# Inverse roots spread by two DMAs through a row in device memory, in place of products with the identity

## The chip, the cores and the metric

The kernel runs on one core of a Trainium2 chip. The metric is the device time of one execution in microseconds; the profile adds the span from the first to the last instruction of a profiled execution. The core has TensorE (PE, with its weight loads as PEld), VectorE (DVE), ScalarE (ACT), GpSimd (POOL) and SyncE (SP), which here only issues DMAs.

## The reference

Two residual layers over x of 512 positions by 1024 channels. Layer 0 is windowed attention, layer 1 is retention with four heads, and each ends in a gated MLP with a causal convolution of width 3. What matters here is where a norm stands:

```python
def rmsnorm(x, g):
    y = xf * lax.rsqrt(jnp.mean(xf * xf, axis=-1, keepdims=True) + EPS)
    return (y * g.astype(jnp.float32)).astype(x.dtype)
...
def retention(h, w_in, w_o):
    q, k, v, g = jnp.split(h @ w_in, [R_QK_COLS, 2 * R_QK_COLS, 2 * R_QK_COLS + R_V_COLS], axis=-1)
...
    o = (of * lax.rsqrt(jnp.mean(of * of, axis=-1, keepdims=True) + EPS)).astype(dt)
    return (jax.nn.silu(g) * o.reshape(B, S, R_V_COLS)) @ w_o

def conv_ffn(h, w_up, conv_w, conv_b, w_down):
    u = h @ w_up
...
    a, b = jnp.split(u, 2, axis=-1)
    return (jax.nn.gelu(a, approximate=False) * b) @ w_down
...
    for i in range(DEPTH):
        h = rmsnorm(x, norm1_g[i])
...
        h = rmsnorm(x, norm2_g[i])
        x = x + conv_ffn(h, ffn_w_up[i], ffn_conv_w[i], ffn_conv_b[i], ffn_w_down[i])
```

A norm's factor is one number for each position, and a product with weights may be taken before the factor is applied.

## The kernel before

Activations lie with channels on the 128 partitions and the 512 positions along the row (x is eight tiles of 128x512). Each operand of a large product is split into a high and a low part (hi and lo), and a product is three matmuls: `mm3` (lines 1237 to 1239). Weights stream from device memory in units of 128x2048 (1 MB) into `raw`, which has two slots s = 0 and 1. ACT makes `w_hi` of a unit and DVE makes `w_lo` (both in functions called `split`), and SP's `load` of the next unit into the same slot waits for that `w_lo` (`w_lo_ok`). Two units are a pair. The order of work on each engine is written out by hand. Engines are tied by counting semaphores: `unit` is PE's wait for `w_lo`, `w_used` and `tile_done` say that PE has finished with a unit or a PSUM bank.

The factor of a norm is applied after the product. Its path is: squares on ACT (`sq`), their sum over tiles (`ssum`), the sum over partitions by four small matmuls (`columns`, line 1254), DVE's `variance` (line 634), POOL's power of -0.5 (`inv_root`, line 1097), which leaves `rcol`: 128 partitions x 4, position t*128+p at partition p, column t. But where channels are on the partitions the factor is wanted as a row of 512 on every partition. `broadcast` (line 1262) makes it: four matmuls of a column of `rcol`, read 128 times over, with the identity, into a free PSUM bank, and ACT's `broadcast_out` (line 341) copies the bank to `rbc`. `rbc[:, 0]` is for norms of x, `rbc[:, 1]` for a head's norm of o.

This is done seven times: for each MLP (ST_F0, ST_F1), for the retention layer (ST_R) and for each of its four heads (ST_HEAD + h). Around them:

- MLP, `up_pair`: PE's unit (0, s=0) fills banks 0 and 1, then come the `columns`; unit (0, 1) fills banks 2 and 3, with the broadcast after its first 12 matmuls; unit (1, 0) takes banks 0 and 1 again and waits for the two `u` of DVE (lines 872 and 874), each a bank times `rbc`. DVE then makes `y` with ACT and the `split` of the pair after.
- Retention, `qkvg(h, first)`: two units for the head's queries and keys (banks 4 to 7), the product with w_o of the head before (`project`), two units for the values (`pv`, banks 4 to 7), scores, and two units for the gate (`gate_part`). For the first head POOL makes `csr`, the rotation's tables times `rbc` (line 1214); DVE's `rotary` (lines 931 to 934) takes banks 4 to 7 times `csr`, and PE's value tiles t = 0 and t = 2 wait for it (`rt_ok`).
- The end of a head on DVE: `gate_in(m)` is a gate bank times `rbc[:, 0]`, `normalised(m)` an output bank times `rbc[:, 1]`, `gated(m)` their product, `o_lo_part(m)` its low part, which `project` waits for (`olo_ok`).

After heads 0 to 2, PE goes to the next head's queries and keys before that head's `project`; after head 3 `project` follows at once.

## Time and profile before

| what | value |
|---|---|
| median of 3 runs | 1275.97 us (1275.8 to 1276.37) |
| the profiled execution | 1275.93 us, its span 1273.8 us |
| PE busy | 1265.5 us (99%) |
| DVE, ACT, POOL busy | 714.4, 468.6, 144.6 us |
| granted TensorE clock | 1.000 of full speed |

The busy time of an engine is its share of the span; what an engine that isn't the bound does, matters only where the bound waits for it.

### The profile page before, as it was taken

The page shows a single profiled execution, that of the slowest core. Times are in us where ns is not written, and L with a number is a line of the kernel's source. Part 1 is how long each engine was busy: PE and PEld are TensorE (multiplying, and loading weights), DVE is VectorE, ACT ScalarE, POOL GpSimd, SP SyncE. Part 2 cuts the span into 40 slices and gives each one's busy share as a digit, 9 for nine tenths or more (in the row PEclk, how much of TensorE's full clock was granted, in tenths as well). Part 3 has the DMA queues.
Part 4 walks back from the last instruction along what each step waited for, and adds up shares of the span by engine and source line. Part 5 has one row for each costly group of instructions (what it writes and reads, how often), then busy time and mean ns, then how long its engine had stood idle before and what let it go on. Part 6 is the DMA issues. An engine that isn't in the chain of part 4 may idle for free.

```text
span 1273.8 us, 15763 instructions
## 1 busy us (share of the span) xinstructions
PE 1265.5 (99%) x5900; PEld 1047.3 (82%) x5900; DVE 714.4 (56%) x906; ACT 468.6 (37%) x655; POOL 144.6 (11%) x138
## 2 busy tenths in 40 slices
PE   9999999999999999999999999999999999999999
PEld 8767888888888888888888888888888888888887
DVE  6776576677664333545535634634677776764221
ACT  6654454444442223233233223223454444442120
POOL 3652300000000001402102201201000000000000
PEclk9999999999999999999999999999999999999999
DMA  6110222222222324322222220311222222222322
GB/s 243 68 67 34 99 100 99 99 88 88 91 80 98 101 91 144 126 69 85 95 83 66 99 99 33 132 67 64 99 99 96 90 88 92 95 78 94 111 91 89
DMA packets 20993, 118.78 MB, mean 93 GB/s; under 512 B 2560, under 2 KB 3584, under 8 KB 10208
## 3 DMA queue, kind: packets, MB, share of 16 engines
q1 hardware_dynamic: 20016, 116.14, 25.9%
q10 hardware_dynamic: 720, 1.85, 0.4%
q8 instruction: 21, 0.34, 0.1%
q0 software_dynamic: 224, 0.35, 0.1%
q14 instruction: 12, 0.10, 0.0%
HBM read 116.23 MB, written 2.10 MB: 93 GB/s over the span
## 4 chain that ended last, share of the span: by engine, by line
PE 96%; POOL 1%; DVE 1%; ACT 1%; DMA 1%; SPq 1%; issue 0%; POOLq 0%
PE ps L1237 31%; PE ps L1239 31%; PE ps L1238 31%; PE ps L1330 1%; PE ps L1339 1%; PE ps L1352 1%; DMA raw<-in_w_q 1%; PE ps L1262 0%; PE ps L1254 0%; ACT qn L365 0%; POOL qs L1130 0%; SPq L277 0%; PE ps L1313 0%; SPq L261 0%; DVE w_lo L621 0%; ACT w_hi L322 0%
## 5 line engine op out<-in xcount | busy, mean ns | idle before, releaser
L1237 PE MATMUL ps<-h_hi,w_hi 128*128 128x512 f32 x960 | 375.2, 391 | 0.0
L1239 PE MATMUL ps<-h_hi,w_lo 128*128 128x512 f32 x960 | 373.5, 389 | 0.0
L1238 PE MATMUL ps<-h_lo,w_hi 128*128 128x512 f32 x960 | 373.5, 389 | 0.0
L621 DVE TENSOR_TENSOR w_lo<-raw,w_hi 128x2048 fp32r<-128x2048 f32 (+1 forms) x115 | 244.8, 2129 | 138.2 <-ACT w_hi L322 138.1
L322 ACT ACTIVATE w_hi<-raw 128x2048 fp32r<-128x2048 f32 (+1 forms) x115 | 202.5, 1761 | 214.1 <-PE ps L1239 214.1
L1239 PEld LDWEIGHTS ps<-h_hi,w_lo 128*128 128x128 f32 x960 | 180.2, 188 | 37.9
L1238 PEld LDWEIGHTS ps<-h_lo,w_hi 128*128 128x128 f32 x960 | 180.3, 188 | 36.6
L1237 PEld LDWEIGHTS ps<-h_hi,w_hi 128*128 128x128 f32 x960 | 180.3, 188 | 36.4
L1237 PE MATMUL ps<-g_hi,w_hi 128*128 128x512 f32 x352 | 136.9, 389 | 0.0
L1238 PE MATMUL ps<-g_lo,w_hi 128*128 128x512 f32 x352 | 136.9, 389 | 0.0
L1239 PE MATMUL ps<-g_hi,w_lo 128*128 128x512 f32 x352 | 136.9, 389 | 0.0
L505 ACT ACTIVATE y<-u,cvec 128x512 f32<-128x512 f32 x88 | 71.4, 816 | 141.5 <-DVE u L872 71.8
L1237 PE MATMUL ps<-w_hi,h_hi 128*128 128x512 f32 (+1 forms) x224 | 85.8, 383 | 0.7 <-DVE w_lo L621 0.7
L1239 PE MATMUL ps<-w_hi,h_lo 128*128 128x512 f32 (+1 forms) x224 | 84.1, 375 | 0.0
L1238 PE MATMUL ps<-w_lo,h_hi 128*128 128x512 f32 (+1 forms) x224 | 84.0, 375 | 0.0
L1238 PEld LDWEIGHTS ps<-g_lo,w_hi 128*128 128x128 f32 x352 | 66.1, 188 | 13.8
L1239 PEld LDWEIGHTS ps<-g_hi,w_lo 128*128 128x128 f32 x352 | 66.1, 188 | 13.7
L1237 PEld LDWEIGHTS ps<-g_hi,w_hi 128*128 128x128 f32 x352 | 66.1, 188 | 13.6
L878 DVE SCALAR_TENSOR_TENSOR y<-u,cvec,y 128x512 f32<-128x512 f32 x88 | 65.6, 748 | 19.5 <-ACT y L505 19.5
L874 DVE TENSOR_TENSOR u<-ps,rbc 128x512 f32<-128x512 f32 x44 | 30.4, 690 | 77.9 <-PE ps L1239 77.9
L511 ACT ACTIVATE g_hi<-gp 128x512 f32 (+1 forms) x44 | 27.8, 632 | 118.3 <-DVE gp L887 118.3
L1086 POOL TENSOR_TENSOR ssum<-sq 128x512 f32<-128x512 f32 x6 | 12.2, 2028 | 482.1 <-ACT sq L533 260.7
(158 smaller groups left out, 1447.8 us busy)
## 6 DMA issues: line engine op xcount, KB each, us to landing
raw<-in_w_up SPq DMA_DIRECT2D x44, 1024.0 KB, 4.8
raw<-in_w_ret SPq DMA_DIRECT2D x32, 1024.0 KB, 4.8
raw<-in_w_dn SPq DMA_DIRECT2D x32, 704.0 KB, 4.0
raw<-in_w_ao SPq DMA_DIRECT2D x4, 1024.0 KB, 4.7
raw<-in_w_q SPq DMA_DIRECT2D x3, 1024.0 KB, 5.3
x<-in_xT SPq DMA_DIRECT2D x8, 256.0 KB, 5.5
out<-x SPq DMA_DIRECT2D x8, 256.0 KB, 4.9
raw<-in_w_q SPq DMA_DIRECT2D x2, 512.0 KB, 6.4
```

The source lines that it names most:

```text
L322: nc.scalar.activation(w_hi[:, s, 0:cols], raw[:, s, 0:cols], ACT.Copy).then_inc(w_hi_ok, 1)
L505: nc.scalar.activation(y[:, ab, :], u[:, ab, 2:S + 2], ACT.Identity, scale=c[:, 0:1], bias=c[:, 1:2]).then_inc(yb_ok, 1)
L511: nc.scalar.activation(g_hi[:, bass.ds(i, 1), :].rearrange("p o f -> p (o f)"), gp[:, :], ACT.Copy).then_inc(ghi_ok, 1)
L621: nc.vector.tensor_tensor(w_lo[:, s, 0:cols], raw[:, s, 0:cols], w_hi[:, s, 0:cols].bitcast(F32), ALU.subtract).then_inc(w_lo_ok, 1)
L874: nc.vector.tensor_tensor(u[:, 1, 2:S + 2], ps[:, 2 * s + 1, :], rbc[:, 0, :], ALU.mult).then_inc(u_ok, 1)
L878: nc.vector.scalar_tensor_tensor(y[:, ab, :], u[:, ab, 1:S + 1], c[:, 4 * ab + 1:4 * ab + 2], y[:, ab, :], ALU.mult, ALU.add).then_inc(y1_ ...
L1237: nc.tensor.matmul(dst, st[0], mv[0], start=start, stop=False)
L1238: nc.tensor.matmul(dst, st[0], mv[1], start=False, stop=False)
L1239: return nc.tensor.matmul(dst, st[1], mv[0], start=False, stop=stop)
L1330: last = nc.tensor.matmul(ps[:, score_bank(g, par), i * P:i * P + nk], qT[rows, n, j:j + 2, :].rearrange("p j q -> p (j q)"), keys[rows, c ...
L1339: last = nc.tensor.transpose(ps[:, TT_BANK, i * P:(i + 1) * P], pn[:, g % 2, i, :], ident[:, :])
L1352: last = nc.tensor.matmul(ps[par * A_DH:(par + 1) * A_DH, PV_BANK, 0:4 * CHUNK], v[:, n // 2, c * A_DH:(c + 1) * A_DH], pT[:, g % 2, par * ...
```

## The change

Six of the seven broadcasts (all but head 3's) no longer use PE, a PSUM bank and ACT. A tensor `root_row` of 512 numbers is added in device memory. SP's new `spread` waits for `rcol` (`r_ok`), writes it to `root_row` by one DMA (512 single numbers of 4 bytes, since positions lie across partitions), waits until that has landed (`row_out`), and reads the row back to all 128 partitions of `rbc` by a second DMA (128 rows of 2 KB, 256 KB in all). The users of `rbc` wait for `row_in` in place of `bc_ok`. Each `spread` stands at a fixed place among SP's loads. Around this:

- In both MLPs, ACT and DVE do the `split` of pair 1, slot 0 before they wait for `rbc`, not after the first `y`.
- At the end of heads 0 to 2, DVE does `gate_in(3)` ahead of `normalised(0)`, and the `split` of the next head's slot 1 behind `gated(0)`, and ACT's `split` is moved with it.
- Head 3 has its own copy of the code (`final`). It keeps the broadcast; on DVE, `o_lo_part(1)` now comes before the wait for PE's last gate unit and `gate_in(3)`.

The diff, cut to its core (left out are the arguments passed down, the tensor's declaration and the loops' bounds, which go from heads 1 to 3 in a loop to heads 1 and 2 in a loop and head 3 behind it):

```diff
-BC_F0, BC_R, BC_HEAD, BC_F1 = 0, 1, 2, 2 + R_HEADS
+ROW_F0, ROW_R, ROW_HEAD, ROW_F1 = 0, 1, 2, 1 + R_HEADS
...
+        row_out, row_in = sem("row_out"), sem("row_in")
@@ -291,8 +292,20 @@
             def rows(src, i):
                 return src[bass.ds(i, 1), :, :].rearrange("o p f -> (o p) f")
 
+            def spread(n, row, which):
+
+                sp.wait_ge(r_ok, n + 1)
+                sp.dma_start(root_row.rearrange("(t p) -> p t", p=P), rcol[:, which, :],
+                             allow_slow_non_contiguous=True).then_inc(row_out, 16)
+                sp.wait_ge(row_out, 16 * row + 16)
+                sp.dma_start(rbc[:, which, :], root_row.unsqueeze(0).to_broadcast([P, S])).then_inc(row_in, 16)
+
             def mlp(layer, w_up, w_dn):
-                with sp.Fori(0, FT // 2) as j:
+                for j in range(2):
+                    for s in range(2):
+                        load(w_up[2 * j + s], PAIR_UP[layer] + j, s, UW)
+                spread(ST_F1 if layer else ST_F0, ROW_F1 if layer else ROW_F0, 0)
+                with sp.Fori(2, FT // 2) as j:
                     for s in range(2):
                         load(rows(w_up, 2 * j + s), PAIR_UP[layer] + j, s, UW)
                 with sp.Fori(0, KT) as j:
@@ -300,9 +313,19 @@
                         load(rows(w_dn, 2 * j + s), PAIR_DN[layer] + j, s, DW)
 
             mlp(0, w_up0, w_dn0)
-            with sp.Fori(0, 4 * R_HEADS) as j:
+            for j in range(2):
                 for s in range(2):
-                    load(rows(w_ret, 2 * j + s), PAIR_RET + j, s, UW)
+                    load(w_ret[2 * j + s], PAIR_RET + j, s, UW)
+            spread(ST_R, ROW_R, 0)
+            for j in range(2, 4):
+                for s in range(2):
+                    load(w_ret[2 * j + s], PAIR_RET + j, s, UW)
+            with sp.Fori(0, R_HEADS - 1) as h:
+                for i in range(4):
+                    for s in range(2):
+                        load(rows(w_ret, 8 * h + 2 * (4 + i) + s), PAIR_RET + 4 * h + 4 + i, s, UW)
+                        if i == 0 and s == 0:
+                            spread(ST_HEAD + h, ROW_HEAD + h, 1)
             mlp(1, w_up1, w_dn1)
             for m in range(KT):
                 sp.wait_ge(xe_ok, XE_DN1 + m + 1)
...
@@ -498,13 +521,14 @@
                     i = 2 * j + s
                     f = FT * layer + i
                     if first and s == 0:
-                        broadcast_out(BC_F1 if layer else BC_F0, 0)
+                        split(up + j + 1, s, cols)
                     for ab in range(2):
                         act.wait_ge(u_ok, 2 * f + ab + 1)
                         c = cvec[:, layer, bass.ds(i, 1), 4 * ab + 2:4 * ab + 4].rearrange("p o f -> p (o f)")
                         nc.scalar.activation(y[:, ab, :], u[:, ab, 2:S + 2], ACT.Identity,
                                              scale=c[:, 0:1], bias=c[:, 1:2]).then_inc(yb_ok, 1)
-                    split(up + j + 1, s, cols)
+                    if not (first and s == 0):
+                        split(up + j + 1, s, cols)
                     act.wait_ge(y_ok, 2 * f + 1)
                     nc.scalar.activation(y[:, 0, :], y[:, 0, :], ACT.Gelu).then_inc(ge_ok, 1)
                     act.wait_ge(gp_ok, f + 1)
@@ -544,7 +568,7 @@
             mlp(0, False)
 
 
-            def qkvg(h, first):
+            def qkvg(h, first, final=False):
 
                 p0 = PAIR_RET if first else PAIR_RET + 4 * h - 1
                 pv = PAIR_RET + 1 if first else p0 + 2
...
@@ -572,13 +596,19 @@
                     act.wait_ge(o_done, 4 * h + m + 1)
                     square(SQ_HEAD + 4 * h, m, ps[:, m, :])
                 gate(h, 2)
-                broadcast_out(BC_HEAD + h, 1, bank=5)
-                for m in range(2):
-                    out_hi(h, m)
-                gate(h, 3)
-                for m in range(2, RV_T):
-                    out_hi(h, m)
-                split(pv + 2, 1, UW)
+                if final:
+                    broadcast_out(1, bank=5)
+                    for m in range(2):
+                        out_hi(h, m)
+                    gate(h, 3)
+                    for m in range(2, RV_T):
+                        out_hi(h, m)
+                    split(pv + 2, 1, UW)
+                else:
+                    split(pv + 2, 1, UW)
+                    gate(h, 3)
+                    for m in range(RV_T):
+                        out_hi(h, m)
 
             def gate(h, m):
                 act.wait_ge(gx_ok, 4 * h + m + 1)
...
@@ -866,8 +896,9 @@
                     c = cvec[:, layer, bass.ds(i, 1), :].rearrange("p o f -> p (o f)")
                     if first and s == 0:
                         variance(ST_F1 if layer else ST_F0, 0, D)
+                        split(up + j + 1, s, cols)
                         dve.wait_ge(cst, 4 + layer)
-                        dve.wait_ge(bc_ok, (BC_F1 if layer else BC_F0) + 1)
+                        dve.wait_ge(row_in, 16 * (ROW_F1 if layer else ROW_F0) + 16)
                     dve.wait_ge(tile_done, td + i + 1)
                     nc.vector.tensor_tensor(u[:, 0, 2:S + 2], ps[:, 2 * s, :], rbc[:, 0, :], ALU.mult).then_inc(u_ok, 1)
                     dve.wait_ge(w_used, 2 * (up + j) + s + 1)
@@ -881,7 +912,8 @@
                         dve.wait_ge(y1_ok, 2 * f + ab + 1)
                         nc.vector.scalar_tensor_tensor(y[:, ab, :], u[:, ab, 0:S], c[:, 4 * ab:4 * ab + 1],
                                                        y[:, ab, :], ALU.mult, ALU.add).then_inc(y_ok, 1)
-                    split(up + j + 1, s, cols)
+                    if not (first and s == 0):
+                        split(up + j + 1, s, cols)
                     dve.wait_ge(ge_ok, f + 1)
                     dve.wait_ge(y_ok, 2 * f + 2)
                     nc.vector.tensor_tensor(gp[:, :], y[:, 0, :], y[:, 1, :], ALU.mult).then_inc(gp_ok, 1)
...
                 dve.wait_ge(g_done, h + 1)
                 gate_in(2)
-                dve.wait_ge(bc_ok, BC_HEAD + h + 1)
-                for m in range(2):
-                    normalised(m)
-                    gated(m)
-                o_lo_part(0)
-                dve.wait_ge(w_used, 2 * (pv + 1) + 2)
-                gate_in(3)
-                o_lo_part(1)
-                normalised(2)
-                gated(2)
-                normalised(3)
-                gated(3)
-                o_lo_part(2)
-                o_lo_part(3)
-                split(pv + 2, 1, UW)
+                if final:
+                    dve.wait_ge(bc_ok, 1)
+                    for m in range(2):
+                        normalised(m)
+                        gated(m)
+                    o_lo_part(0)
+                    o_lo_part(1)
+                    dve.wait_ge(w_used, 2 * (pv + 1) + 2)
+                    gate_in(3)
+                    for m in range(2, RV_T):
+                        normalised(m)
+                        gated(m)
+                    o_lo_part(2)
+                    o_lo_part(3)
+                    split(pv + 2, 1, UW)
+                else:
+                    dve.wait_ge(w_used, 2 * (pv + 1) + 2)
+                    gate_in(3)
+                    dve.wait_ge(row_in, 16 * (ROW_HEAD + h) + 16)
+                    normalised(0)
+                    gated(0)
+                    split(pv + 2, 1, UW)
+                    normalised(1)
+                    gated(1)
+                    o_lo_part(0)
+                    normalised(2)
+                    gated(2)
+                    o_lo_part(1)
+                    normalised(3)
+                    gated(3)
+                    o_lo_part(2)
+                    o_lo_part(3)
 
             def add_head(h, s, e, p):
 
...
@@ -1209,7 +1259,7 @@
             inv_root(ST_R, 0)
 
             pool.wait_ge(r_in, 32)
-            pool.wait_ge(bc_ok, BC_R + 1)
+            pool.wait_ge(row_in, 16 * ROW_R + 16)
             for i in range(2):
                 nc.gpsimd.tensor_tensor(csr[:, i, :], tab[:, i, :], rbc[:, 0, :], ALU.mult).then_inc(csr_ok, 1)
 
@@ -1506,9 +1556,6 @@
                                 pe.wait_ge(h_ready, KT * norm + k + 1)
                             c = (ab * KT + k) * P
                             last = mm3(ps[:, 2 * s + ab, :], weights(s, c, c + P), hidden(k), k == 0, k == KT - 1)
-                            if first and s == 1 and ab == 0 and k == 3:
-
-                                broadcast(ST_F1 if layer else ST_F0, 0)
                         last.then_inc(w_used if ab else tile_done, 1)
                         if first and s == 0 and ab == 1:
                             columns(ST_F1 if layer else ST_F0, SQ_BASE[norm] + KT)
...
@@ -1553,12 +1600,10 @@
                             pe.wait_ge(gx_ok, 4 * (h - 1) + 2 * s + e + 1)
                             if s == 0 and e == 0:
                                 pe.wait_ge(var_ok, ST_HEAD + h)
-                            if s == 0 and e == 1:
-                                pe.wait_ge(bc_ok, BC_HEAD + h)
                         elif s == 0:
                             pe.wait_ge(xe_ok, XE_DN0 + 7 + e)
-                        if first and s == 1 and e == 1:
-                            pe.wait_ge(bc_ok, BC_R + 1)
+                        if first and s == 1 and e == 0:
+                            pe.wait_ge(var_ok, ST_R + 1)
                         for k in range(KT):
                             if first and s == 0 and e == 0:
                                 pe.wait_ge(h_ready, KT * NORM_R + k + 1)
@@ -1568,8 +1613,6 @@
                             last.then_inc(w_used, 1)
                         if first and s == 0 and e == 0:
                             columns(ST_R, SQ_BASE[NORM_R] + KT)
-                        if first and s == 0 and e == 1:
-                            broadcast(ST_R, 0)
                 if not first:
                     project(h - 1, p0 + 1)
                 pv = PAIR_RET + 1 if first else p0 + 2
@@ -1617,9 +1660,12 @@
                 pe.wait_ge(gx_ok, 4 * h + 2)
                 columns(ST_HEAD + h, SQ_HEAD + 4 * (h + 1), bank=4)
                 gate_part(2, 6, KT).then_inc(g_done, 1)
-                gate_part(3, 0, 1)
-                broadcast(ST_HEAD + h, 1, bank=5)
-                gate_part(3, 1, KT).then_inc(w_used, 1)
+                if final:
+                    gate_part(3, 0, 1)
+                    broadcast(ST_HEAD + h, 1, bank=5)
+                    gate_part(3, 1, KT).then_inc(w_used, 1)
+                else:
+                    gate_part(3, 0, KT).then_inc(w_used, 1)
 
```

How the rows stand on the engines: a row is the line, the operation, out<-in, the shape, and the semaphores that it waits for.

On DVE at the start of the first MLP, before. `u` is a product bank times `rbc`, `w_lo` the low part of weights:

```order
L634 TENSOR_SCALAR var<-ps 128x4 [waits col_done]
L872 TENSOR_TENSOR u<-ps,rbc 128x512 [waits tile_done,bc_ok,cst]
L874 TENSOR_TENSOR u<-ps,rbc 128x512 [waits w_used]
L878 SCALAR_TENSOR_TENSOR y<-u,cvec,y 128x512 [waits yb_ok] x2
L882 SCALAR_TENSOR_TENSOR y<-u,cvec,y 128x512 [waits y1_ok] x2
L621 TENSOR_TENSOR w_lo<-raw,w_hi 128x2048 [waits w_hi_ok]
L887 TENSOR_TENSOR gp<-y 128x512 [waits y_ok,ge_ok]
```

The same place on DVE in the change:

```order
L664 TENSOR_SCALAR var<-ps 128x4 [waits col_done]
L651 TENSOR_TENSOR w_lo<-raw,w_hi 128x2048 [waits w_hi_ok]
L903 TENSOR_TENSOR u<-ps,rbc 128x512 [waits tile_done,row_in,cst]
L905 TENSOR_TENSOR u<-ps,rbc 128x512 [waits w_used]
L909 SCALAR_TENSOR_TENSOR y<-u,cvec,y 128x512 [waits yb_ok] x2
L913 SCALAR_TENSOR_TENSOR y<-u,cvec,y 128x512 [waits y1_ok] x2
L919 TENSOR_TENSOR gp<-y 128x512 [waits y_ok,ge_ok]
```

`w_lo` moved from behind the four `y` to ahead of the first `u`, whose wait is now for the row.

On SP around the retention layer's norm, in the change (before, there is one loop of `in_w_ret` loads and nothing else):

```order
L275 DMA raw<-in_w_ret 128x2048 [waits w_lo_ok] x4
L298 DMA root_row<-rcol 128x4x1 [waits r_ok]
L301 DMA rbc<-root_row 128x512 [waits row_out]
L275 DMA raw<-in_w_ret 128x2048 [waits w_lo_ok] x4
```

The two DMAs of the row stand behind the first four of the layer's loads, and the next four behind them.

On DVE at the end of head 3 before (the loop's code for heads 1 to 3), from the gate's third bank on; `sg<-ps,rbc` is `gate_in`, `rt<-ps,rbc` is `normalised`, `sg<-rt,sg` is `gated`:

```order
L994 TENSOR_TENSOR o_lo<-sg,o_hi 128x512 [waits ohi_ok]
L981 TENSOR_TENSOR sg<-ps,rbc 128x512 [waits w_used]
L994 TENSOR_TENSOR o_lo<-sg,o_hi 128x512 [waits ohi_ok]
L985 TENSOR_TENSOR rt<-ps,rbc 128x512 [waits sq_ok]
L990 TENSOR_TENSOR sg<-rt,sg 128x512 [waits on_ok,sg_ok]
```

The same place in the change's own code for head 3:

```order
L1022 TENSOR_TENSOR sg<-rt,sg 128x512 [waits on_ok,sg_ok]
L1026 TENSOR_TENSOR o_lo<-sg,o_hi 128x512 [waits ohi_ok] x2
L1013 TENSOR_TENSOR sg<-ps,rbc 128x512 [waits w_used]
L1017 TENSOR_TENSOR rt<-ps,rbc 128x512 [waits sq_ok]
L1022 TENSOR_TENSOR sg<-rt,sg 128x512 [waits on_ok,sg_ok]
```

The second `o_lo` moved ahead of the wait for `w_used` and of the last `gate_in`.

## Rows read from the trace of the kernel before

**Rows 1.** The page: span, busy times, and the chain's shares by engine

```profile
span 1273.8 us, 15763 instructions
PE 1265.5 (99%) x5900; PEld 1047.3 (82%) x5900; DVE 714.4 (56%) x906; ACT 468.6 (37%) x655; POOL 144.6 (11%) x138
PE 96%; POOL 1%; DVE 1%; ACT 1%; DMA 1%; SPq 1%; issue 0%; POOLq 0%
```

**Rows 2.** PE's waits: who waited for whom, us in total, times, longest

```profile
PE ps L1237 <- DVE qn L703: 1.4, 1, 1.4
...
PE ps L1237 <- DVE o_lo L994: 0.7, 1, 0.7
```

**Rows 3.** Timeline of PE around the retention broadcast: start, us, instruction, count

```profile
512.31 0.39 PE L1237 MATMUL ps<-h_hi,w_hi 128*128 128x512 f32 x1
...
516.85 0.39 PE L1239 MATMUL ps<-h_hi,w_lo 128*128 128x512 f32 x1
517.07 1.05 PE L1262 MATMUL ps<-ident,rcol 128*128 128x128 f32 x8
...
518.20 0.39 PE L1238 MATMUL ps<-h_lo,w_hi 128*128 128x512 f32 x1
```

**Rows 4.** Timeline of PE, DVE and ACT at the end of head 3

```profile
885.76 0.63 ACT L589 ACTIVATE o_hi<-sg 128x512 fp32r<-128x512 f32 x1 [0.76 <-DVE sg L990]
...
887.25 0.39 PE L1239 MATMUL ps<-o_hi,w_lo 128*128 128x512 f32 x1
...
887.61 0.68 DVE L994 TENSOR_TENSOR o_lo<-sg,o_hi 128x512 fp32r<-128x512 f32 x1
...
888.35 0.50 PE L1237 MATMUL ps<-o_hi,w_hi 128*128 128x512 f32 x1 [0.70 <-DVE o_lo L994]
888.69 0.40 PE L1238 MATMUL ps<-o_lo,w_hi 128*128 128x512 f32 x1
```

**Rows 5.** Stretch 1254.5 to 1259.5, a store of 256 KB: DMA share in 40 slices, packets, landing

```profile
DMA  0000000000000000000000889995000000000000
q1 hardware_dynamic: 144, 0.26, 13.8%
out<-x SPq DMA_DIRECT2D x1, 256.0 KB, 2.0
```

**Rows 6.** Stretch 0 to 3, DMA queue of ACT: packets, MB, share of 16 engines

```profile
q10 hardware_dynamic: 103, 0.01, 2.7%
```

**Rows 7.** Stretch 511.8 to 517, the 1 MB load before the retention row: issue, DMA slices

```profile
511.83 0.33 SPq L274 DMA_DIRECT2D raw<-in_w_ret  x1
DMA  0000000959009309999494998959799114000000
```

**Rows 8.** All loads of x: DMA to landing

```profile
DMA to landing us min/median/max: 3.0/5.5/5.6
```

**Rows 9.** Timeline of POOL, DVE and PE at the start of retention

```profile
509.37 2.29 DVE L621 TENSOR_TENSOR w_lo<-raw,w_hi 128x2048 fp32r<-128x2048 f32 x1 [1.58 <-ACT w_hi L322]
...
512.58 1.01 POOL L1097 TENSOR_TENSOR rcol<-var,mhalf 128x4 f32<-128x4 f32 x1 [3.63 <-DVE var L634]
...
518.90 2.55 POOL L1214 TENSOR_TENSOR csr<-rt,rbc 128x512 f32<-128x512 f32 x2 [5.31 <-ACT rbc L341]
...
523.96 2.41 DVE L621 TENSOR_TENSOR w_lo<-raw,w_hi 128x2048 fp32r<-128x2048 f32 x1
...
528.88 0.39 PE L1237 MATMUL ps<-w_hi,h_hi 128*128 128x512 f32 x1
```

**Rows 10.** Timeline at the first MLP's start: POOL's root, PE's unit (1, 0)

```profile
156.53 1.01 POOL L1097 TENSOR_TENSOR rcol<-var,mhalf 128x4 f32<-128x4 f32 x1 [6.84 <-DVE var L634]
...
168.01 0.39 PE L1237 MATMUL ps<-h_hi,w_hi 128*128 128x512 f32 x1
```

**Rows 11.** Timeline after head 0: POOL's root, PE's next unit of slot 1

```profile
578.32 1.01 POOL L1097 TENSOR_TENSOR rcol<-var,mhalf 128x4 f32<-128x4 f32 x1 [2.06 <-DVE var L634]
...
596.60 0.39 PE L1237 MATMUL ps<-h_hi,w_hi 128*128 128x512 f32 x1
```

25 lines of the change are left out of this document (14 added, 11 removed).

## The prediction

> **What bounds the kernel now.** I read the page first. PE is busy 1265.5 us of a span of 1273.8 us, and the chain that ended last is 96% PE [rows 1]; no other engine passes 56%. So time can be won only by taking work off PE or by closing its gaps, and lost only by making a new gap. The list of PE's waits came next: the longest in the whole run is 1.4 us, in attention, and the one place that the change touches is 0.7 us behind an `o_lo` of DVE [rows 2]. Then I read the timeline around each broadcast, to see what it takes of PE and how much slack its users have. The sum is made against the profiled execution, 1275.93 us; the median of the three runs is 1275.97, 0.04 more.
>
> **Six broadcasts gone from PE.** Ahead of the retention broadcast, twenty matmuls after that of 512.31 comes the one of 516.85: a pace of 0.227 us each. The broadcast starts at 517.07, and the second matmul behind it at 518.20 [rows 3]. Without it that second one would start at 516.85 + 2 x 0.227 = 517.30, so one broadcast costs 0.90 us. All seven do the same work; six go: 6 x 0.90 = **-5.4 us**. Their six copies on ACT and the PSUM banks are worth nothing: ACT is never what PE waits for there.
>
> **Head 3.** PE starts a matmul at 887.25 and the next at 888.35, then 888.69 [rows 4]. At the pace they would be at 887.48 and 887.70: 0.99 us lost, because `o_lo_part(1)` runs from 887.61, behind `gate_in(3)`, although its input was there at 885.76 + 0.63 = 886.39. In the new order it runs at once and ends near 887.1, 0.3 us before PE wants it. What is late next: `gate_in(3)` and what follows it start 0.1 us later than before at most (0.68 for the moved piece, less the 0.6 that it no longer takes behind), while PE wants `normalised(2)` only at 886.80 + 12 x 0.227 = 889.5. **-1.0 us**.
>
> **How long the row takes.** The trace has no write of single numbers, so both ends are bounded. A store of 256 KB moves data for six slices of 0.125 (0.75 us) and lands 2.0 after issue [rows 5]: 1.25 us is fixed. Its 144 packets take 13.8% of 16 engines for 5 us, 77 ns each, and up to 0.75 / 8 = 94 ns each as they follow one another. The small packets of ACT's queue at the start, of 128 bytes, take 2.7% of 16 engines for 3 us over 103 of them, 13 ns each [rows 6]. The write has 512 numbers, 32 for each of the 16 engines: from 32 x 13 ns = 0.4 to 32 x 94 ns = 3.0 us, so it lands L = 1.65 to 4.25 us after issue. Neither row is nearer (one has the size, the other the direction), so I take the middle, L = 2.95. The read back is 256 KB: 2.0 by that store, 3.0 by the fastest load of x [rows 8]. I take 2.3, nearer the store, since nothing else is on the queue then. Each SP step starts 0.17 after what releases it (a load is issued at 511.83, behind a `w_lo` that ended at 511.66 [rows 7, 9]). From `rcol` to `rbc`: 0.17 + 2.95 + 0.17 + 2.3 = 5.6 us.
>
> The Trainium skill, "DMA: Bandwidth & Descriptors", section "Anatomy of one DMA", gives 2.0 us + bytes / 436e3. By it, called an estimate, the write is 2.0 and the read back 2.6, and the sum below would be 0.25 us better. No run here shows it; for the 256 KB store the trace has 2.0, not 2.6.
>
> **The two MLPs.** `rcol` is there at 156.53 + 1.01 = 157.54. PE enters unit (1, 0) at 168.01 [rows 10], 0.9 earlier without the broadcast: 167.1. It wants the first `u` (0.69) by then: 157.54 + 0.17 + L + 0.17 + 2.3 + 0.1 + 0.69 + 0.06 = 161.03 + L. L may be 6.1; there are 3.1 us to spare. The first `u` starts at about 163.2. What stands behind DVE's wait is the rest of that first tile, which PE wants only a unit later. The moved `split` (1.9 us on ACT, 2.3 on DVE) runs inside the row's 5.6 us. The second MLP repeats these distances. SP's next load waits behind the row by about 3 us, and is wanted more than 10 us later. **0**.
>
> **The start of retention** is where the row is tight. `rcol` is ready at 513.59 [rows 9], but on SP's queue the row's write stands behind a 1 MB load issued at 511.83, whose first packets show 0.9 later (the 8th slice of 0.13), whose data fills the slices to about 516.0 [rows 7]. If the write's data follows that load's, it lands at 516.0 + (L - 0.9). If it isn't held up, at 513.76 + L, 1.3 earlier. Taking the first: `csr` starts at 515.1 + L + 0.17 + 2.3 + 0.1 = 517.7 + L, for L = 2.95 at 520.65, against 518.90 before. Queued behind `csr` on DVE are four products of `rotary` and then the `split` of the value weights, which ended 7.47 us after `csr` began (523.96 + 2.41 = 526.37). PE enters the value unit, which waits for it, at 528.88, now 527.98. So `csr` may start at 520.45, that is L up to 2.75. The stall is 0.2 us at L = 2.95, 0 at the low end, and 1.5 + 0.7 = 2.2 with both DMAs at their high ends. Unqueued it is 0. **+0.2 us**.
>
> The Trainium skill, same page, section "Queues, rings and completion order", says that a DMA engine serves the rows of its rings in turn and each row in order; by that rule the write does queue behind the load, as I took it. No row here shows a small DMA behind a large one.
>
> **Heads 0 to 2.** `rcol` is ready at 579.33 [rows 11], so `rbc` is there near 585.0, while PE goes on for two units with the next head. Behind DVE's wait for the row stand `normalised(0)`, `gated(0)` (1.5 us) and the `split` (2.29) of slot 1, which PE wants at 596.60 - 0.9 = 595.7. So the row may come as late as 591.8, L = 9.8. The rest of the head's tail is wanted by `project` another unit later. SP's load behind the row waits for that same `split` anyway. The loads here land before the row is due. **0**.
>
> The extra code for head 3 costs PE nothing that I can price: PE shows no wait at any loop's edge.
>
> **The sum.** 1275.93 - 5.4 - 1.0 + 0.2 = 1269.7, and 0.04 up to the median: **1269.8 us**, 0.5% less.
>
> **The rivals.** All are put against a bound of 0.2% (2.55 us), about what this kernel's measurement can tell from no change.
>
> - *The retention row is late by more.* Were both DMAs near their high ends, or 1 to 2 us beyond, PE would wait 2 to 3.8 us for `w_lo` at the value unit and nowhere else: 1271.5 to 1273.4. For it: the slack is a few tenths. Against it: both must be slow at once.
> - *Slower: the write of single numbers is slow.* The stalls add to (L - 2.75) + 2 x (L - 6.1) above L = 6.1. They eat the gain of 6.4 at L = 7.1, that is at 0.18 us for each number, and pass +0.2% at L = 8.0: L = 9 gives 1281. For it: such a write isn't in the trace, and each number is a transfer of its own to device memory. Against it: it is twice what a 2 KB packet takes. The Trainium skill, same page, "Specifications", has it that below 512 bytes the engine reads, modifies and writes, which is how it could come about.
> - *The gain goes to a place I don't see* (a DMA that delays a weight load, instruction code of the longer program), or L lies between 6 and 8: within 0.2%.
> - *The forecast*: stall at retention from 0 to 2 us, 1269.3 to 1271.5.
>
> **How the numbers follow.** The forecast has 0.74, the late retention row 0.10, no difference 0.08, slower 0.08. The first two make faster 0.84. The range begins at 1269.0 (no stall, and 0.6 for the spread of runs and a broadcast read too short by some hundredths) and ends at 1272.8, inside the second case.
>
> **What would show it.** In the changed kernel's profile: one broadcast left (8 of the 56 matmuls of that kind, PE's busy time down by about 5 to 6 us); no wait of PE on `o_lo` at head 3; the write landing 1.7 to 4.3 us after issue and the read back 2 to 3; a first `u` near 163; `csr` near 520 to 521, with at most a few tenths of PE waiting for DVE's `w_lo` right before the value unit; the tail of heads 0 to 2 ending near 596. The prediction is wrong if the write takes over 6 us, or if PE shows waits behind `u` or `w_lo` in the MLPs, which cost twice.

## The result, and the profile after

The changed kernel takes **1299.18 us** (median of 6 runs, 1298.22 to 1300.01) against 1275.88 in the same comparison: a ratio of 1.0182, 95% interval 1.0171 to 1.0192. It is 23.3 us slower, where 6.2 us faster was predicted. Its profiled execution has a span of 1297.7 us, 23.9 more than before, and those 23.9 are explained below.

The page of the changed kernel (compare [rows 1]); the third row gives the chain's shares by engine:

```profile
span 1297.7 us, 15539 instructions
PE 1269.8 (98%) x5852; PEld 1046.8 (81%) x5852; DVE 713.4 (55%) x906; ACT 464.8 (36%) x649; POOL 144.8 (11%) x138
PE 83%; DMA 7%; DVE 4%; issue 3%; POOL 3%; ACT 1%; POOLq 0%; DVEq 0%; ACTq 0%
```

The chain is the work that ended last, followed back from the last instruction; it was 96% PE. 13 points of it have gone elsewhere, 6 of them to DMA (1% before, 7% now). PE has 48 products fewer, and yet its busy time is 4.3 us longer.

PE's waits in the changed kernel (compare [rows 2]): who waited for whom, us in total, times, longest:

```profile
PE ps L1287 <- DVE u L903: 10.9, 2, 5.5
PE ps L1287 <- DVE w_lo L651: 10.0, 8, 6.5
PE ps L1287 <- DVE qn L733: 1.4, 1, 1.4
```

The first two rows make 20.9 us in ten places. Before, PE waited for no `u`, and for `w_lo` 0.7 us in one place; `o_lo` is gone from the list. DVE isn't slow there, it waits itself. This is DVE's list in the changed kernel, and POOL's with it:

```profile
DVE u L903 <- DMA rbc<-root_row: 24.3, 2, 12.2
DVE rt L1017 <- DMA rbc<-root_row: 21.5, 3, 7.4
POOL csr L1264 <- DMA rbc<-root_row: 13.4, 1, 13.4
```

The two new DMAs, by tile, in the changed kernel: all six writes of the row and all six reads of it, ns of the issue, first and last start, and then us to landing over all twelve. A DMA has landed when the semaphore that its user waits for has its full count.

```profile
L298 SPq DMA_DIRECT2D root_row<-rcol x6: 377/380/386, 157.5 to 939.4; - x6
L301 SPq DMA_DIRECT2D rbc<-root_row x6: 320/326/333, 167.0 to 947.7; - x6
...
DMA to landing us min/median/max: 3.2/7.2/10.4
```

The same view for the six reads alone:

```profile
DMA to landing us min/median/max: 3.2/4.6/6.1
```

So the writes hold the upper half. One by one, from the stretch around each, the writes took 9.5 (first MLP), 8.7 (retention), 10.4, 8.3 and 10.4 (heads) and 8.3 us (second MLP). The timeline of SP at the first MLP shows it: the read can only be issued when the write has landed.

```profile
157.54 0.39 SPq L298 DMA_DIRECT2D root_row<-rcol  x1
167.03 0.33 SPq L301 DMA_DIRECT2D rbc<-root_row  x1
```

Now the surprise. These are the DMA slices of 0.25 us from 157 to 167, the first ten us of that write, and the packets of the queue in them:

```profile
DMA  0000008100000000000000000000000000000000
q1 hardware_dynamic: 528, 0.00, 2.5%
```

The 528 packets (the 512 numbers and 16 more) are all in the seventh and eighth slices, over by 159.0, 1.5 us after the issue. The landing comes 8 us later, and in between no DMA engine shows any work. Over the six writes this gap runs from 6.3 to 9.1 us. What the engines' time can tell of such a write is not when it lands.

At retention a 1 MB load was issued 2.1 us ahead of the write, at 518.95. These are the slices of 0.1 us from 521 to 525, busy share and GB/s; the write was issued at 521.06:

```profile
DMA  9799797998979599799097892000000000000000
GB/s 410 328 573 410 328 573 328 410 573 328 410 328 573 246 492 492 328 492 492 1 248 6 6 168 2 0 0 0 0 0 0 0 0 0 0 0 0 0 0 0
```

The load fills them to 522.9. The write's packets, busy slices with next to no bytes, only show from there to 523.5, together with the load's last ones. So they start 1.9 us after the issue, where the other five writes' start about 0.9 after it: the small write stood behind the large load, as the prediction took it. It landed 8.7 us after issue even so, within the range of the others.

The consequence in the first MLP, in the changed kernel's timeline of PE (compare 168.01 of [rows 10]):

```profile
166.83 0.39 PE L1289 MATMUL ps<-h_hi,w_lo 128*128 128x512 f32 x1
172.62 0.79 PE L1287 MATMUL ps<-h_hi,w_hi 128*128 128x512 f32 x1 [5.41 <-DVE u L903]
173.21 0.63 PE L1288 MATMUL ps<-h_lo,w_hi 128*128 128x512 f32 x1
```

Behind the wait the products are slow as well: each takes 0.63 us against 0.39, and the next starts 0.43 after it against 0.23. The stretches of 5 us show why: length, busy times of PE, PEld, DVE, ACT and POOL, then PEclk, the granted clock as a share of full speed.

```profile
165.00:170.00 5.00, 2.21 (x10) 1.50 (x8) 0.00 (x0) 0.00 (x0) 0.00 (x0) 1.00 0.08 34
170.00:175.00 5.00, 2.38 (x6) 1.90 (x7) 2.84 (x5) 2.38 (x3) 0.00 (x0) 0.62 0.57 229
175.00:180.00 5.00, 5.00 (x17) 3.98 (x16) 3.91 (x7) 2.64 (x5) 0.00 (x0) 0.70 0.00 0
180.00:185.00 5.00, 5.00 (x23) 4.13 (x22) 5.00 (x6) 2.91 (x3) 0.00 (x0) 1.00 0.00 0
```

PE had stood still from 167 to 172.6, and then for part of two stretches it had the lower level, 1.2 instead of 2.4 GHz (17 products in 5 us where 23 are usual). The same happens at the other two long waits (0.50 in 540 to 545 at retention, 0.53 in 955 to 960 in the second MLP). In the three places 35 products start 7.4 us later in all than they would at the full pace, which is most of PE's longer busy time. What it costs in the end is another question, which the run with filled waits answers.

**Where the 23.9 us are.** Each norm's column product on PE is a milestone. In the changed kernel they start at (left out are those of heads 1 and 2):

```profile
155.27 0.95 PE L1304 MATMUL ps<-ones,ssum 128*128 128x1 f32 x8
517.99 0.95 PE L1304 MATMUL ps<-ones,ssum 128*128 128x1 f32 x8
592.45 0.95 PE L1304 MATMUL ps<-ones,ssum 128*128 128x1 f32 x8
...
895.87 0.95 PE L1304 MATMUL ps<-ones,ssum 128*128 128x1 f32 x8
937.13 0.95 PE L1304 MATMUL ps<-ones,ssum 128*128 128x1 f32 x8
```

From the same rows of the other kernels (their experiments follow), the us between milestones, and in the last line from the last milestone to the span's end:

| Stretch | before | rows left out | changed | waits filled | sums by four |
|---|---|---|---|---|---|
| up to the first MLP's | 155.3 | 155.3 | 155.3 | 155.5 | 155.0 |
| first MLP | 355.4 | 354.5 | 362.7 | 362.6 | 354.5 |
| retention's start, to head 0's | 66.4 | 65.4 | 74.5 | 72.9 | 67.0 |
| to head 3's (three heads) | 301.1 | 298.3 | 303.4 | 305.7 | 299.8 |
| head 3's end | 42.3 | 41.3 | 41.3 | 41.3 | 42.0 |
| second MLP and end | 353.3 | 352.4 | 360.6 | 359.2 | 352.6 |

Against the version in which nobody waits for a row, the change loses 8.2 in each MLP, 9.0 at retention's start and 5.1 over three heads, 30.5 in all. That version gains 6.6 on before. 30.5 - 6.6 = 23.9.

### The profile page after: what moved, and what is told of

Read it like the earlier page. It is cut to its first block, busy times and chain, and to the rows that moved or that the text cites. A ratio compares the mean times of both kernels' runs of the same rounds, so it can differ in the third digit from the quotient of the medians.

```text
span 1297.7 us, 15539 instructions
## 1 busy us (share of the span) xinstructions
PE 1269.8 (98%) x5852; PEld 1046.8 (81%) x5852; DVE 713.4 (55%) x906; ACT 464.8 (36%) x649; POOL 144.8 (11%) x138
## 4 chain that ended last, share of the span: by engine, by line
PE 83%; DMA 7%; DVE 4%; issue 3%; POOL 3%; ACT 1%; POOLq 0%; DVEq 0%; ACTq 0%
PE ps L1287 27%; PE ps L1289 27%; PE ps L1288 27%; DMA root_row<-rcol 4%; DMA rbc<-root_row 2%; DVE w_lo L651 1%; PE ps L1380 1%; PE ps L1389 1%; POOL ssum L1139 1%; PE ps L1402 1%; DVE rt L1017 1%; POOL ssum L1136 1%; POOL rcol L1147 0%; DVE sg L1022 0%; DMA dec<-in_decay 0%
## 5 line engine op out<-in xcount | busy, mean ns | idle before, releaser
L1287 PE MATMUL ps<-h_hi,w_hi 128*128 128x512 f32 x960 | 377.3, 393 | 13.3 <-DVE u L903 10.9
L528 ACT ACTIVATE y<-u,cvec 128x512 f32<-128x512 f32 x88 | 71.4, 817 | 166.2 <-DVE u L903 100.7
```

What stands on the lines that cost most here:

```text
L528: nc.scalar.activation(y[:, ab, :], u[:, ab, 2:S + 2], ACT.Identity, scale=c[:, 0:1], bias=c[:, 1:2]).then_inc(yb_ok, 1)
L1287: nc.tensor.matmul(dst, st[0], mv[0], start=start, stop=False)
```

## The experiments

**The DMAs by themselves.** The kernel before, with ten DMAs twice over behind its last store, each waited for before the next. The core of the edit:

```diff
+            for _ in range(2):
+                timed(row.rearrange("(t p) -> p t", p=P), rcol[:, 0, :], True)
+                timed(row.rearrange("(p t) -> p t", t=PT), rcol[:, 0, :])
+                timed(row.rearrange("(t p) -> p t", p=P)[:, 0:1], rcol[:, 0, 0:1], True)
+                timed(wide.rearrange("(t p) f -> p t f", p=P)[:, :, 0:1], rcol[:, 0, :].unsqueeze(2), True)
...
```

> The kernel before, with twenty DMAs behind the last store, each waited for before the next is issued (ten kinds, twice). Nothing else is on the queue. Single numbers: the write's 8.3 to 10.4 us to landing come from the 512 separate four-byte writes, so 512 numbers land in about 9 us whether packed or spaced, 128 numbers or 128 pieces of 16 bytes in about a quarter of the excess over the 2.0 us of a 256 KB store (3 to 4 us). Shared lines: it comes from several DMA engines writing into the same stretch of memory, so 512 numbers spaced 512 bytes apart land in 2 to 3 us, the packed ones in 9. Any small write: everything under 512 bytes a piece takes 8 to 9 us, only the 128 x 512 B and 128 x 2 KB writes about 2. For the read back: if the shared source row is what makes it 3.2 to 6.1 us, the read of one row by 128 partitions takes over 3 us here too and the read of 128 different rows about 2; if it was the load issued behind it, both take 2 to 2.5.

Its DMA issues, bytes each and median us to landing:

```profile
wide<-rcol SPq DMA_DIRECT2D x2, 2.0 KB, 2.7
...
row<-rcol SPq DMA_DIRECT2D x2, 0.5 KB, 7.8
```

From issue to issue, the change's own write took 9.3 and 8.3 us in the two rounds, the same 2 KB as 128 pieces of 16 bytes (four neighbouring positions from one partition) 1.8 and 2.7. 128 single numbers took 7.8 in the median, so a quarter of the count takes off little. 512 single numbers of which each is 512 bytes from the next took 2.7, so their size isn't it either, and small pieces aren't slow as such: 128 pieces of 64 and of 512 bytes took 1.4 and 1.5. What is left is that separate numbers are neighbours in memory. For the read back, one row read by 128 partitions took 3.0, and 128 different rows 2.7: the shared source isn't what makes it 3.2 to 6.1 in the kernel.

**How near is too near.** The same frame, with the spacing of 128 numbers varied, and the read back right behind the writes.

> The kernel before, followed by two rounds of 12 DMAs, each waited for on SP before the next is issued; the kernel's own work is the same. Six write 128 single numbers (one a partition) at a spacing of 4, 8, 16, 32, 64 and 512 bytes in device memory, one writes 8 bytes a partition packed, then the change's write (512 numbers, packed) with a read of the row by all partitions right behind it, the same with 16 bytes a partition, and a write of the 512 numbers into one partition of SBUF instead of device memory. Theory of neighbours (a number that shares a short stretch of memory with numbers from other partitions is slow): 4 bytes apart about 7.8 us to landing, falling as the spacing grows, and 2.7 or less from 64 bytes on; 8 bytes packed lies between 2.5 and 7.8. Rival, that a piece of 4 bytes is slow by itself: all spacings near 7.8. For the read: if fresh numbers delay it, it lands in 4 us or more behind the change's write and in 3.0 behind the write of 16-byte pieces; if the load on the queue delayed it in the changed kernel, both land in 3.0. SBUF: under 3 us if the slowness is that of device memory, near 8 if it is that of small pieces.

SP's timeline in the first round, from the packed write on. Each start is the landing of the DMA ahead:

```profile
1294.50 0.38 SPq L316 DMA_DIRECT2D row<-rcol  x1
1304.26 0.33 SPq L316 DMA_DIRECT2D rbc<-row  x1
1309.40 0.32 SPq L316 DMA_DIRECT2D row<-rcol  x1
1310.81 0.32 SPq L316 DMA_DIRECT2D rbc<-row  x1
1315.00 0.56 SPq L316 DMA_DIRECT2D raw<-rcol  x1
```

The change's write: 9.8 us, the read behind it 5.1. The write of 16-byte pieces: 1.4, the read behind it 4.2. The second round has 10.9, 3.9, 2.4 and 3.1. 512 numbers into one partition of SBUF took 1.9 in the median of two: single numbers are not slow there. From issue to issue the spacings gave, in the two rounds:

| 128 single numbers, apart by | 4 bytes | 8 | 16 | 32 | 64 | 512 |
|---|---|---|---|---|---|---|
| us, first and second round | 7.5, 7.5 | 4.5, 4.8 | 1.6, 2.3 | 1.6, 1.8 | 1.4, 1.5 | 1.4, 1.4 |

Packed pieces of 8 bytes took 3.3. So the price falls steeply up to 16 bytes and is gone at 64. Each number here comes from another partition; single numbers of one partition, written side by side, weren't tried, so whether it matters that the partitions differ stays open. Both probes are single runs, of two rounds each. The read's share is less clear: 5.1 and 3.9 behind the change's write, 4.2 and 3.1 behind the other. It is 0.8 and 1.0 slower in the two rounds, but the rounds differ by more.

**All row work left out.** The changed kernel without write, read and the waits for them; the first six inverse roots don't reach the products.

```diff
-                spread(ST_F1 if layer else ST_F0, ROW_F1 if layer else ROW_F0, 0)
-            spread(ST_R, ROW_R, 0)
-                            spread(ST_HEAD + h, ROW_HEAD + h, 1)
-            pool.wait_ge(row_in, 16 * ROW_R + 16)
...
```

> The change without its row: no write, no read back, and no wait for them, so that the users of the row multiply by what lies in it (the inverse roots are left out of six norms). Theory that the prediction's sum was right and only the row's length was wrong: 1269.5 us, 6.4 less than before, and no wait of PE over 0.3 us at the six places. Rival, that the new order on DVE and ACT or the longer program costs something itself: 1272 or more, with PE waiting for w_lo or u although the row is free.

Measured: 1269.1 us, ratio 0.9945 (0.993 to 0.996). PE's longest wait for `w_lo` is 0.5. The gains that the prediction adds up are there in full, 6.9 us.

**Head 3's order alone.** The kernel before, with `o_lo_part(1)` ahead of the wait and `gate_in(3)`:

```diff
+                o_lo_part(1)
                 dve.wait_ge(w_used, 2 * (pv + 1) + 2)
                 gate_in(3)
-                o_lo_part(1)
```

> The kernel before with one line moved: o_lo_part(1) ahead of the last gate_in, for all heads. By the prediction's term for head 3: 1.0 us less than before (1274.9), and the wait of PE for o_lo gone. Rival, that the wait only moves to normalised(2) or to o_lo_part(2): 0 to 0.3 less.

Measured: 1274.88 us, 1.1 less than the 1276.01 beside it, ratio 0.999 (0.9981 to 0.9999). All four heads of this kernel have the new order, but the 0.7 of [rows 2] is a single wait, and it is gone. The interval only just leaves out 1: by it the 1.1 may be anything from 0.1 to 2.4.

**The heads alone by rows.** The change, with the broadcast put back in both MLPs and at retention's start:

```diff
-                spread(ST_F1 if layer else ST_F0, ROW_F1 if layer else ROW_F0, 0)
-            spread(ST_R, ROW_R, 0)
+                            if first and s == 1 and ab == 0 and k == 3:
+                                broadcast(ST_F1 if layer else ST_F0, 0, 7)
...
```

> The change with the broadcasts of both MLPs and of the retention norm restored as before; only heads 0 to 2 go by the row. If the loss sits at the two MLPs and at the start of retention, this is faster than before: 3 x 0.90 for the broadcasts and 1.0 for head 3, less 1 to 2 us of waiting at a head whose write takes over 9.8 us: 1272.5 to 1274. If the heads lose too (their write lands in up to 10.4 us), 1276 or more.

Measured: 1276.57, ratio 1.0004 (0.9995 to 1.0013): the heads' part gains nothing. Their row, in this kernel's timeline of SP, and who waited for it:

```profile
579.34 0.39 SPq L299 DMA_DIRECT2D root_row<-rcol  x1
587.51 0.33 SPq L302 DMA_DIRECT2D rbc<-root_row  x1
...
592.54 0.69 DVE L1024 TENSOR_TENSOR rt<-ps,rbc 128x512 f32<-128x512 f32 x1 [6.88 <-DMA rbc<-root_row]
...
596.37 0.49 PE L1294 MATMUL ps<-h_hi,w_hi 128*128 128x512 f32 x1 [0.55 <-DVE w_lo L654]
```

The row is there at 592.5, not 585; my own limit was 591.8, and PE loses 0.8 us there and some 0.5 more at the projection. From one head's column product to the next it is 100.7 to 100.9 in this kernel, where before has 100.4 and the version without rows 99.4. I had expected 1272.5 to 1274 because I judged a head by its write alone (late above 9.8, with the read back at the prediction's 2.3); the write took 8.2 to 8.5, but with a read back of 4.5 to 5.0 the sum of both is past the 12.1 allowed.

**Pieces of 16 bytes.** The column product takes its positions four apart, so that each partition of `rcol` holds four neighbours and the row goes out as 128 pieces of 16 bytes. First with retention's norm by its broadcast, then with all six by rows.

```diff
-                    last = nc.tensor.matmul(ps[:, bank, t:t + 1], ssum[:, t * P:(t + 1) * P], ones[:, :],
+                    st = ssum.rearrange("p (q t) -> p t q", t=PT)[:, t, :] if packed else ssum[:, t * P:(t + 1) * P]
-                sp.dma_start(root_row.rearrange("(t p) -> p t", p=P), rcol[:, which, :],
+                    sp.dma_start(root_row.rearrange("(p t) -> p t", t=PT), rcol[:, which, :]).then_inc(row_out, 16)
```

> The changed kernel, but the column product takes its positions four apart, so that a partition of rcol holds four neighbouring positions and the row is written as 128 pieces of 16 bytes, not 512 of 4; this in both MLPs and heads 0 to 2, while the norm of retention goes back to its broadcast on PE. Theory (the write's landing is what cost): it lands in 2.5 instead of 8.3 to 10.4, PE waits nowhere for u or w_lo, five broadcasts at 0.9 and the 1.1 of head 3 are gained, 1276.0 - 4.5 - 1.1 = 1270.4 us. With the read back at 5 us instead of 3: still under 0.3 us of stalls. Rival (the two DMAs and their queue are slow in this place whatever their shape): stalls behind u in both MLPs as in the changed kernel, 1285 or more.

> As the other packed version, with the norm of retention by the row too (all six, as in the change, but written as 16-byte pieces). Theory: 1269.1 (all rows left out) plus what the row of retention is late by: with a write of 2.5 and a read back of 3.0, about 0.4; with a read back of 4.5, 2.0. So 1269.3 to 1271.3 us, with a wait of PE for w_lo at the first value unit of up to 2 us. Rival (the 1 MB load ahead on the queue holds the row's write back by more): a wait of 3 us or more there, 1272 or more.

Measured: 1274.9 us, ratio 0.9992 (0.9983 to 1.0001), and 1275.22, ratio 0.9994 (0.9985 to 1.0003). The stalls are gone by the form of the write, with the column product that it needs, 24 us against the changed kernel: it lands after 1.4 and 2.1 us in the median, the read after 4.3 and 4.2, and PE waits for no `u`. But the first is 4.5 us above what I expected, the second 3.9 to 5.9. The reason stands in the timeline of PE in the first of the two:

```profile
155.36 1.80 PE L1309 MATMUL ps<-ones,ssum 128*128 128x1 f32 x8
157.02 0.47 PE L1291 MATMUL ps<-h_hi,w_hi 128*128 128x512 f32 x1
```

From the column product to the next product it is 1.66 us. In the version without rows it is 156.11 - 155.30 = 0.81. The same tile's weight loads in the packed kernel, ns minimum, median and maximum over all norms, those without a stride among them:

```profile
L1309 PEld LDWEIGHTS ps<-ones,ssum x64: 188/309/329, 23.9 to 920.8; 128*128 128x128 f32 x64
```

A load with a stride of 16 bytes takes 0.329 us, where 0.192 is the median before. PE pays 0.85 for each norm: 5 x 0.85 = 4.25, and 1270.4 + 4.25 = 1274.65. My edit had a cost that I hadn't looked for.

The second version says something of the prediction too. At retention its row took 2.8 + 3.9 = 6.7 us from the write's issue, with the write again behind the 1 MB load, and PE waited for nothing there. Each of its stretches is 0.9 longer for each strided column product in it than with the rows left out, and no more: with a quick write all six rows are free.

**The waits filled.** The changed kernel with idle products where PE waits longest:

```diff
+                fill(23, 7)
...
+                if first:
+                    fill(27, 0)
```

> The changed kernel with idle products of PE put where it waits: 23 in each MLP behind the first pair (5.2 us into a free bank) and 27 ahead of the first value unit of retention (6.1 us). They add no result. Theory (each long wait also costs clock behind it: granted 0.50 to 0.62 for some 5 us): the waits behind u and w_lo shrink to under 1 us each, the granted clock stays at 1.00 through all three places, and 8 to 9 us come back: 1299.2 - 8.5 = 1290.7 us. Rival (the slow products behind the waits are not from the wait, but from the data or the banks): the slow stretches stay and the time is 1299 or more.

Measured: 1301.54, ratio 1.0199 (1.0185 to 1.0213), nothing won. Its five runs spread from 1299.23 to 1301.88, and the profiled one, from which the table's column and what follows are read, is the quickest of them. The granted clock is 1.00 in all its stretches, so that half of the theory holds, but not the other. The timeline of DVE and PE in the first MLP says why:

```profile
173.00 0.69 DVE L903 TENSOR_TENSOR u<-ps,rbc 128x512 f32<-128x512 f32 x1 [13.00 <-DMA rbc<-root_row]
...
183.74 2.29 DVE L651 TENSOR_TENSOR w_lo<-raw,w_hi 128x2048 fp32r<-128x2048 f32 x1
...
186.17 0.49 PE L1287 MATMUL ps<-h_hi,w_hi 128*128 128x512 f32 x1 [1.21 <-DVE w_lo L651]
```

PE, at full clock, runs up against DVE again, which has worked from the row's landing on with pauses of 0.7 us at most and still has a tile's chain ahead of the next `w_lo`. In the changed kernel DVE starts at 171.87 and has the same `w_lo` at 182.61, both 1.1 us earlier; PE comes to it slowly and doesn't wait. The slow clock for the most part fills time in which PE would wait for DVE. By the table of stretches the filled version wins 0.1 in the first MLP, 1.6 at retention and 1.4 in the second MLP, not the 8 to 9 that I expected. Its rows differed: after the column product they came 0.9 and 0.6 later at the first two and 0.5 earlier at the third, so the clock may have cost 1.0, 2.2 and 0.9. That is an estimate of some 4 us for the clock's part of the 23.9, from one profiled execution of each. The heads took 2.3 more, and so did PE's waits in them (5.5 against 3.2), behind writes of 11.3, 8.7 and 11.4 us.

**The MLPs alone by the change's write.** The first of the two packed versions, but with the change's write of single numbers in the MLPs:

```diff
-                spread(ST_F1 if layer else ST_F0, ROW_F1 if layer else ROW_F0, 0, True)
+                spread(ST_F1 if layer else ST_F0, ROW_F1 if layer else ROW_F0, 0)
```

(and with it their column products without a stride).

> Only the two MLPs by the row of single numbers, as in the change; heads 0 to 2 by the 16-byte row, retention's norm by its broadcast. It prices the MLPs alone. Without stalls it would take what the version with 16 bytes everywhere took less the two strided column products: 1274.9 - 1.7 = 1273.2. Theory (the row's time decides: write 8.3 to 9.5 and read back 4.8 to 6.1, against 8.4 allowed for both, then DVE's chain catching up): 8.2 for each MLP, as between the column products of the changed kernel, 1289.6 us. Rival (the MLPs in the change paid for what retention and the heads did to the queue or the clock): less than 5 each, under 1283.

Measured: 1288.73, ratio 1.0102 (1.0087 to 1.0118), 0.9 off. Against 1273.2 the two MLPs pay 15.5, 7.8 each. The price is theirs and owes nothing to the form of the rows at retention and the heads.

**The stride moved off PE.** All six by rows of 16-byte pieces; the squares are summed through a view that puts every fourth position together, so the column products are as before.

```diff
+        sums = ssum.rearrange("p (t q) -> p t q", t=PT)
...
-                    nc.vector.tensor_tensor(ssum[:, :], ssum[:, :], sq[:, m % 2, :], ALU.add).then_inc(ssum_ok, 1)
+                    nc.vector.tensor_tensor(sums, sums, fours(sq[:, m % 2, :]), ALU.add).then_inc(ssum_ok, 1)
```

> All six roots by a row of 16-byte pieces, as in the packed version, but the column products read their weights without a stride again: the squares are summed (POOL, in the second MLP DVE) through a view that puts every fourth position together, so the stride lies in the operands of those additions. Theory (the packed versions lost their gain to the strided weight loads, 1.66 instead of 0.81 us per column product on PE): six times 0.85 come back from the 1275.2 of the version with all six, 1275.2 - 5.1 = 1270.1 us, with column products of 0.95 us busy and no wait of PE over 1.5 us in the touched places. Rival (the strided additions take as much longer, or the packed versions lose elsewhere): additions over 2.1 us on POOL, or the time stays at 1274 to 1276.

Measured: **1272.64 us**, ratio 0.9976 (0.9966 to 0.9985), 3.3 us below before and the fastest version with nothing left out. The column products are back at 0.95, but 2.5 us are missing. The waits of PE in this kernel:

```profile
PE ps L1317 <- POOL ssum L1151: 1.2, 3, 0.5
PE ps L1300 <- DVE w_lo L660: 1.0, 2, 0.6
PE ps L1300 <- DVE h_lo L665: 0.9, 2, 0.5
```

And POOL's additions, ns minimum, median and maximum:

```profile
L1151 POOL TENSOR_TENSOR ssum<-ssum,sq x20: 1286/1564/1987, 133.0 to 874.2; 128x512 f32<-128x512 f32 x20
```

The additions take 1.56 us in the median where they took 1.29, on DVE 1.09 instead of 0.68; after the heads PE now waits for the sum. Those waits are 1.2 us; that the rest of the 2.5 comes from the longer additions as well wasn't shown. Both theories were partly right: the stride costs less there than on PE, but not nothing. In both MLPs the row itself is free, within 0.2 us of the version that waits for none (354.5 and 352.6 in the table).

## Why the prediction was wrong

**The step that failed** is "How long the row takes": "it lands L = 1.65 to 4.25 us after issue", of which I took 2.95. It landed after 8.3 to 10.4. Both ends were made from the time that packets take on the DMA engines, and that time was, if anything, too long: all of them were over 1.5 us after issue, or 2.4 behind the load. What I had wrong is the rest, above all the time from the last packet to the landing. I took 1.25 us for all of it as fixed, from the one store of 256 KB [rows 5]; here the last packet alone is 6.3 to 9.1 us ahead of the landing. That single packets are cheap in [rows 6] said nothing of this, since those are loads into SBUF, where 512 single numbers land in 1.9 us in the probe as well. The probes, with nothing else on the queue, show that it is this pattern, and not the size or the queue, and only in part the number: 7.5 us for 128 numbers side by side and 9.8 to 10.9 for 512 in the same probe, 1.4 for 128 at 64 bytes. Why neighbours wait so long for their landing, no run shows.

The Trainium skill, "Perfetto Trace Analysis", section "DMA Instruction — HWDGE (DVE, Sync)", has it that an engine's last descriptor increments the semaphore once the write before it is confirmed. The trace agrees: 528 packets by 159.0, the release at 167.0. The rule of the Trainium skill that the rival cites, from "DMA: Bandwidth & Descriptors", section "Specifications", makes every piece below 512 bytes a read, modify and write. By it alone single numbers would be as slow 64 bytes apart as side by side; they take 1.4 and 7.5, so it doesn't tell the two apart, and the measurement decides. The formula of the Trainium skill that the prediction gives beside its bounds, from section "Anatomy of one DMA" of the same page, stands there for DMAs issued by GpSimd, while these come from SP. As an estimate it gives 2.0 us for the write, which took 8.3 to 10.4.

**The read back** was also mis-sized: 2.3 with 3.0 as its upper end, and it measured 3.2 to 6.1. In the three versions with all or most rows in 16-byte pieces it is 3.0 to 5.4. This term was wrong, but with a quick write it would have cost nothing: in the version with all six of them PE waits at none.

**The allowances held.** The prediction lets write and read together take 6.1 + 2.3 = 8.4 in an MLP; they took 14.3 and 14.4, and PE waited 5.4 and 5.5. At retention 5.05 were allowed beyond the 1.3 that the prediction counts for the load ahead, so 6.4 from issue, and 13.2 taken; that is 6.8 too much, and PE waited 6.5. In the heads 9.8 + 2.3 = 12.1 were allowed, and 13.1 to 13.7 taken.

**The rival on the other side** was the right one, in where the stalls fall and with its point of break-even (L = 7.1), and had 8 in 100; how it says that the write could come to be slow is answered above. Its price was too low. With the measured writes (9.5 and 8.3 in the MLPs; 8.7 at retention, less the 1.3 for the load) its formula gives stalls of 4.6 + 3.4 + 2.2 = 10.2, and 1279.8. Three things were missing. The reads took 2.2, 2.5 and 3.8 more than the 2.3 assumed, 8.5 in all. The heads weren't in it, and paid 5.1. And a wait ends, but the lateness doesn't: the table has 8.2 for each MLP and 9.0 for retention, where allowances and measured times give 5.9, 6.0 and 6.8, so 2.2 to 2.3 more in each, 6.7 in all. 1279.8 + 8.5 + 5.1 + 6.7 = 1300.1, and 0.5 less because the gain was 6.9 and not 6.4, against 1299.2 measured. The last two terms are read off the table, so that the sum closes is no test of them.

Those 6.7 have two parts. The slow products alone would explain them, with 2.4 to 2.6 us in each place, and I first put them to the clock. With the waits filled the clock is 1.00 and only some 4 us come back by the estimate above: about all at retention, less than half in each MLP. The rest there is DVE, which comes out of the wait with a tile's work still ahead of the next `w_lo`.

Two small slips of the prediction change nothing: its rival at L = 9 comes to 1281.6 by its own formula, not 1281, and the formula for a DMA's time would have made the sum 0.2 better, not 0.25.

**What was right**: six broadcasts and head 3 together, 6.4 predicted, 6.9 measured without the rows; head 3 alone 1.0 predicted, 1.1 measured. Nothing unseen took a share. The slack counted for the rows was right too: with 16-byte pieces no row costs PE anything, as the prediction has it but for 0.2 us at retention.

**What stays open**: why the read back takes 3 to 6 us. In the probes it is 3.0 when nothing was written just before, and 3.1 to 5.1 behind a write, with too few samples to say more. Also why each head pays 1.3 to 2.0 when its row is 1.0 to 1.6 late: the two waits of the heads' version show where, not how they add up. Nor was it tried to gather the row in one partition of SBUF first, into which single numbers go in 1.9 us, and write it from there.

## What to carry to other kernels

When a DMA is on a path that somebody waits for, the time of its packets is a floor, not an estimate: ask when it is confirmed, and measure that pattern by itself, with a handful of DMAs behind a kernel's last store, before counting on slack. Don't write to device memory in single numbers side by side; here pieces of four neighbours instead of one made 24 us of difference. And look where a layout change puts its stride: on the weights of PE, the engine that bounds this kernel, it cost 0.85 us a norm, in the sums about half of that (the 2.5 us missing, over six norms).

## What the runs showed of the hardware

- 128 single numbers, one from each partition, written into device memory: 7.5 us to landing at 4 bytes apart, 4.5 to 4.8 at 8, 1.6 to 2.3 at 16, 1.4 to 1.5 at 64. 512 of them side by side take 8.2 to 11.4 over all runs. Into one partition of SBUF 512 of them land in 1.9.
- The DMA engines show nothing of that time: in the first MLP they are idle from 159.0 to 167.0.
- A 2 KB write behind a 1 MB load on the same queue: its packets start 1.9 us after issue instead of 0.9, behind the load's.
- Weight loads of 128 x 128 float32 with a stride of 16 bytes: 0.329 us, packed 0.192. The same stride in an addition of 128 x 512: on DVE 1.09 instead of 0.68 us, on POOL 1.56 instead of 1.29 in the median.
- PE that stood still for 5.4 to 6.5 us had the 1.2 GHz level for some 5 us of work after; with the wait filled by idle products it had 2.4 GHz throughout, and the kernel was no faster (1301.5 against 1299.2).
